# The stick-breaking key sums as two one-pass triangles, the new x turned by transposes, and a shorter Newton step

## What is computed

```python
# branch A, stick-breaking attention, 6 heads of 64, z = q.k * scale (query x key)
log_beta = log_sigmoid(z)
log_one_minus = where(past, log_sigmoid(-z), 0.0)
between = cumsum(log_one_minus, axis=keys, reverse=True) - log_one_minus
a = where(past, exp(log_beta + between), 0.0)
...
x = x + g1 * rms_norm(y, g_post_mix)
h = rms_norm(x, g_pre_ffn) * (1.0 + sc2) + sh2      # the "new x", normed
y = swiglu(h, w_up, w_down)
x = x + g2 * rms_norm(y, g_post_ffn)
```

## Time and profile before

| | |
|---|---|
| median of 3 runs | 461.66 us (461.51 to 461.84) |
| profiled execution, its own time | 461.65 us |
| its span | 459.9 us |
| granted TensorE clock, mean | 0.997 of full |
| TensorE busy | 444.4 us, 97% |
| VectorE busy | 328.5 us, 71% |
| ScalarE busy | 239.2 us, 52% |
| POOL busy | 34.9 us, 8% |
| the six triangles on `tri` (line 1708), with the six on `neg1` (line 1709) | 12 and 12 records, 126.7 to 167.1 us |
| the turns of x (line 1647) | 32 records, 258.6 to 272.1 us |

### The profile page before, as it was taken

One profiled execution on the slowest core, in us unless ns is written; L12 is line 12 of the kernel. 1 busy time (PEld: TensorE's weight loads), 2 busy tenths in 40 slices (PEclk: granted clock), 3 DMA queues, 4 the chain that ended last, 5 costly groups with the idle time before them and its releaser, 6 DMA issues.

```text
span 459.9 us, 7891 instructions
## 1 busy us (share of the span) xinstructions
PE 444.4 (97%) x2982; PEld 390.7 (85%) x2982; DVE 328.5 (71%) x587; ACT 239.2 (52%) x417; POOL 34.9 (8%) x77
## 2 busy tenths in 40 slices
PE   4899999999999999999999999999999999999994
PEld 3678988999999889989997899888888888888883
DVE  4724668786987868856995685796596587678645
ACT  4513884656756655596563576433534525425331
POOL 2000102000322231000000001000000000000000
PEclk9999999999999999999999999999999999999998
DMA  8999466886787657746669425988648557530002
GB/s 289 383 376 331 150 230 224 278 286 238 254 289 275 218 152 273 239 144 201 192 204 370 162 78 166 378 300 276 223 162 288 188 195 261 182 137 0 0 0 91
DMA packets 61634, 99.86 MB, mean 217 GB/s; under 512 B 3892, under 2 KB 44452, under 8 KB 61604
## 3 DMA queue, kind: packets, MB, share of 16 engines
q1 hardware_dynamic: 56480, 81.57, 52.5%
q0 software_dynamic: 4960, 17.84, 11.2%
q10 hardware_dynamic: 164, 0.05, 0.0%
HBM read 98.40 MB, written 1.05 MB: 216 GB/s over the span
## 4 chain that ended last, share of the span: by engine, by line
PE 91%; DVE 4%; issue 2%; ACT 2%; DMA 1%; SPq 0%; DVEq 0%; ACTq 0%
PE psum L1552 17%; PE psum L1951 16%; PE psum L1553 16%; PE psum L1554 16%; PE psum L1952 8%; PE psum L1614 3%; PE psum L1898 3%; PE psum L1568 2%; PE psum L1737 1%; DVE wlo L1094 1%; DMA xt<-in_x_dram 1%; PE psum L1676 1%; PE psum L1674 1%; PE psum L1708 1%; PE psum L1647 1%
## 5 line engine op out<-in xcount | busy, mean ns | idle before, releaser
L1951 PE MATMUL psum<-hcut,whi 128*128 128x512 f32 x320 | 113.6, 399 | 0.0
L1952 PE MATMUL psum<-hcut,wlo 128*128 128x256 f32 x320 | 89.9, 281 | 0.0
L1552 PE MATMUL psum<-hcut,whi 128*128 128x256 f32 x280 | 82.3, 294 | 0.3 <-DVE wlo L1094 0.3
L1553 PE MATMUL psum<-hcut,whi 128*128 128x256 f32 x280 | 79.1, 283 | 0.0
L1554 PE MATMUL psum<-hcut,wlo 128*128 128x256 f32 x280 | 79.1, 282 | 0.0
L1094 DVE TENSOR_TENSOR wlo<-raw,whi 128x768 fp32r<-128x768 f32 (+3 forms) x68 | 64.3, 972 | 19.1 <-ACT whi L743 18.8
L1951 PEld LDWEIGHTS psum<-hcut,whi 128*128 128x128 f32 x320 | 60.1, 188 | 14.9
L1952 PEld LDWEIGHTS psum<-hcut,wlo 128*128 128x128 f32 x320 | 60.5, 189 | 0.4
L743 ACT ACTIVATE whi<-raw 128x768 fp32r<-128x768 f32 (+3 forms) x68 | 55.6, 850 | 6.6 <-PE psum L1862 3.2
L1552 PEld LDWEIGHTS psum<-hcut,whi 128*128 128x128 f32 x280 | 53.4, 191 | 5.5 <-ACT qk L822 2.0
L1553 PEld LDWEIGHTS psum<-hcut,whi 128*128 128x128 f32 x280 | 53.5, 191 | 0.0
(11 more groups left out here) (245 smaller groups left out, 823.9 us busy)
## 6 DMA issues: line engine op xcount, KB each, us to landing
raw<-in_w_up_dram SPq DMA_DIRECT2D x22, 1024.0 KB, 7.6
xn<-in_w_ada_dram POOLq DMA_DIRECT2D x32, 512.0 KB, 5.2
raw<-in_w_in_dram SPq DMA_DIRECT2D x6, 2048.0 KB, 9.1
draw<-in_w_down_dram SPq DMA_DIRECT2D x11, 1024.0 KB, 5.0
ada<-in_w_ada_dram SPq DMA_DIRECT2D x16, 384.0 KB, 9.3
raw<-in_w_in_dram SPq DMA_DIRECT2D x3, 1536.0 KB, 8.8
raw<-in_w_o_dram SPq DMA_DIRECT2D x8, 512.0 KB, 5.2
raw<-in_w_in_dram SPq DMA_DIRECT2D x3, 1280.0 KB, 6.7
```

Source lines behind the costliest of these rows:

```text
L1552: pe.matmul(dst, a[0], b[0], start=first, stop=False)
L1553: pe.matmul(dst, a[0], b[1], start=False, stop=False)
L1951: pe.matmul(dst[:, :], wh, hcut[:, k, :, :].rearrange("p a s -> p (a s)"), start=k == 0, stop=False)
L1952: mm = pe.matmul(dst[:, S:2 * S], wl, hhi[:, k, :], start=False, stop=k == KC - 1)
```

## The change

Three parts. **Sums:** `tri` becomes float32r, a float32r copy `neg_all` of `neg1` is made by ScalarE at the start, and the masked softplus is cut into high part (ScalarE, into the place of `bufa[n % 2]`) and rest (VectorE, in the place of `bufp[n % 2]`). The two float32 matmuls become four float32r ones: each of the two parts by `tri` and by `neg_all`. -1 and 0 have no rest, so nothing is lost on their side. `second` waits for `sp_lo` in place of `sp_masked`. As `bufa` is now in use until the sums are made, two waits on `sums` are added. **New x:** `scale_new_x` replaces `spread_root`. VectorE scales the first 512 columns of the new x and ScalarE the last 512, into `xn`, and `turn_x` transposes the eight chunks of `xn`. **Newton:** ScalarE makes -var/2 by one more single-column Copy after its root, and VectorE's three instructions become two.

```diff
--- before.py
+++ after.py
@@ -292,7 +292,6 @@
         xn = sb("xn", [P, TT, D])
         hx = xn[:, :, :].rearrange("p t (k n) -> p t k n", n=P)
         ada_part = [xn[:, t, :] for t in range(TT)]
-        diag = [xn[:, t, D - P:D] for t in range(TT)]
         gpart, gsum = [xn[:, t, :] for t in range(TT)]
         h32 = xn[:, :, :].rearrange("p t (k n) -> p (t k) n", n=S)
         ident = sb("ident", [P, P])
@@ -306,7 +305,7 @@
         ssq = sb("ssq", [P, 8, 2])
-        var, root_, rinv = (sb(name, [P, 8]) for name in ("var", "root", "rinv"))
+        var, minus_half, root_, rinv = (sb(name, [P, 8]) for name in ("var", "minus_half", "root", "rinv"))
         warm = sb("warm", [P, 1])
         grow = [None, sb("grow1", [KC, P])]
         ones = sb("ones", [P, P], F32R)
@@ -324,7 +323,8 @@
         mrow = sb("mrow", [P, BANK], scope=mix)
         dist = sb("dist", [P, CAUSAL], scope=mix)
         dsel = sb("dsel", [P, CAUSAL], scope=mix)
-        tri = sb("tri", [P, P], scope=mix)
+        tri = sb("tri", [P, P], F32R, scope=mix)
+        neg_all = sb("neg_all", [P, P], F32R, scope=mix)
         neg1 = sb("neg1", [P, P], scope=mix)
         vec_rows = sb("vec_rows", [VEC_END, P], scope=mix)
         score = sb("score", [P, CAUSAL], scope=mix)
@@ -351,10 +351,17 @@
+
+
+        cut_part = ExitStack()
+        sb("cut_pad", [P, TT * D + (3 * KC + N_OCH + FULL_OCH) * S + 2 * D + BANK + 4 * CAUSAL + 4 * P + 2 * TT * 8 + VEC_END],
+           scope=cut_part)
+        sp_cut = [[sb(f"sp_{name}{i}", [P, CAUSAL], F32R, scope=cut_part) for i in range(2)] for name in ("hi", "lo")]
+        cut_part.close()
         start = ExitStack()
         ada = sb("ada", [P, KC, 2, ADA_COLS], scope=start)
...
@@ -641,15 +648,14 @@
             pool.wait_ge(consts, 1)
             pool.affine_select(out=ident[:, :], in_=ident[:, :], compare_op=ALU.not_equal, fill=1.0,
                                base=0, pattern=[[-1, P]], channel_multiplier=1).then_inc(ident_ready, 1)
-            pool.memset(tri[:, :], -1.0).then_inc(consts, 1)
             pool.memset(neg1[:, :], -1.0).then_inc(consts, 1)
             pool.iota(bufa[0][:, 0:P].bitcast(mybir.dt.int32), pattern=[[1, P]], base=0, channel_multiplier=-1).then_inc(consts, 1)
             pool.iota(bufa[0][:, P:CAUSAL].bitcast(mybir.dt.int32), pattern=[[1, 2 * P]], base=-P, channel_multiplier=-1).then_inc(consts, 1)
-            pool.wait_ge(consts, 5)
-            pool.affine_select(out=tri[:, :], in_=tri[:, :], compare_op=ALU.is_ge, fill=0.0,
+            pool.wait_ge(consts, 4)
+            pool.affine_select(out=tri[:, :], in_=neg1[:, :], compare_op=ALU.is_ge, fill=0.0,
                                base=0, pattern=[[-1, P]], channel_multiplier=1).then_inc(consts, 1)
             pool.tensor_copy(dist[:, :], bufa[0][:, :].bitcast(mybir.dt.int32)).then_inc(consts, 1)
-            pool.wait_ge(consts, 7)
+            pool.wait_ge(consts, 6)
             for c0 in (0, 2 * P):
                 pool.affine_select(out=dist[:, c0:c0 + P], in_=dist[:, c0:c0 + P], compare_op=ALU.is_ge, fill=MASKED,
                                    base=0, pattern=[[-1, P]], channel_multiplier=1).then_inc(consts, 1)
@@ -764,6 +770,7 @@
                 act.wait_ge(var_ready, j + 1)
                 act.activation(root_[:, j:j + 1], var[:, j:j + 1], ACT.Sqrt).then_inc(sqrt_ready, 1)
+                act.activation(minus_half[:, j:j + 1], var[:, j:j + 1], ACT.Copy, scale=-0.5).then_inc(half_ready, 1)
             def load_roots():
@@ -879,8 +886,9 @@
                     act.activation(chunk_view(whi, end_hi, k), chunk_view(raw, None, k), ACT.Copy).then_inc(w_hi, 2)
                     chunk_h_hi(k)
                 if k == 2:
-                    act.wait_ge(consts, 3)
+                    act.wait_ge(consts, 2)
                     act.activation(ones[:, :], neg1[:, :], ACT.Copy, scale=-1.0).then_inc(ones_set, 1)
+                    act.activation(neg_all[:, :], neg1[:, :], ACT.Copy).then_inc(ones_set, 1)
                 if k == KC - 1:
                     act.preload_act_table_set("natural_log_exp_and_others")
             for q in range(4):
@@ -902,11 +910,15 @@
                     z = bank[z_place(n)][:, 0:CAUSAL]
                     e = bufa[n % 2][:, :]
                     if n >= 2:
-                        act.wait_ge(sp_ready if n - 2 in SB_NO else p_ready, (SB_NO[n - 2] + 1) if n - 2 in SB_NO else SOFT_NO[n - 2] + 1)
+                        act.wait_ge(sums if n - 2 in SB_NO else p_ready, (SB_NO[n - 2] + 1) if n - 2 in SB_NO else SOFT_NO[n - 2] + 1)
                     then(act.activation(e, z, ACT.Abs))
                     then(act.activation(e, e, ACT.Exp, scale=-1.0))
                     act.activation(e, e, ACT.Ln, bias=1.0).then_inc(ln_ready, 1)
                 take_unit(u)
+                if u in NORM_AT and NORM_AT[u] in SB_NO:
+                    n = NORM_AT[u]
+                    act.wait_ge(sp_masked, 2 * (SB_NO[n] + 1))
+                    act.activation(sp_cut[0][n % 2][:, :], bufp[n % 2][:, :], ACT.Copy).then_inc(sp_hi, 1)
                 if u in LOGIT_PAIR_AT:
                     for h in (2 * LOGIT_PAIR_AT[u], 2 * LOGIT_PAIR_AT[u] + 1):
@@ -1015,13 +1027,20 @@
                     square_sum(3 + 2 * t, n, xt[:, t, BANK * n:BANK * (n + 1)], squares[n])
                 root(3 + 2 * t)
+            def scale_new_x(t):
+                j = 3 + 2 * t
+                act.wait_ge(rinv_ready, t + 1)
+                act.activation(xn[:, t, BANK:D], xt[:, t, BANK:D], ACT.Copy, scale=rinv[:, j:j + 1]).then_inc(xn_other, 1)
+
             squares = [f[:, :, :].rearrange("p j n -> p (j n)") for f in flo]
             norm_y(0, 0)
             norm_new_x(0)
+            scale_new_x(0)
             second_up_hi(0)
             norm_y(0, 1)
             norm_new_x(1)
             second_up_hi(2)
+            scale_new_x(1)
             second_up_hi(3)
             modulate(1)
             for t in range(TT):
@@ -1101,7 +1120,7 @@
             def inverse_root(j, meanwhile=lambda: None):
-                v, r, t = var[:, j:j + 1], rinv[:, j:j + 1], root_[:, j:j + 1]
+                v, half, r, t = [a[:, j:j + 1] for a in (var, minus_half, rinv, root_)]
                 dve.wait_ge(ss_ready, 2 * j + 1)
                 then(dve.tensor_scalar(v, ssq[:, j, 0:1], 1.0 / D, EPS, ALU.mult, ALU.add))
                 dve.wait_ge(ss_ready, 2 * j + 2)
@@ -1109,13 +1128,14 @@
                 meanwhile()
                 dve.wait_ge(sqrt_ready, j + 1)
                 then(dve.reciprocal(r, t))
-                then(dve.tensor_scalar(t, v, r, r, ALU.mult, ALU.mult))
-                then(dve.tensor_scalar(t, t, -0.5, 1.5, ALU.mult, ALU.add))
-                then(dve.tensor_scalar(r, r, t, None, ALU.mult))
-
-            def spread_root(j, t):
-
-                dve.tensor_scalar(diag[t], ident[:, :], rinv[:, j:j + 1], None, ALU.mult).then_inc(xn_ready, 1)
+                dve.wait_ge(half_ready, j - 1)
+                then(dve.tensor_scalar(t, half, r, r, ALU.mult, ALU.mult))
+                then(dve.tensor_scalar(r, t, 1.5, r, ALU.add, ALU.mult))
+
+            def scale_new_x(j, t):
+
+                dve.sem_inc(rinv_ready, 1)
+                dve.tensor_scalar(xn[:, t, 0:BANK], xt[:, t, 0:BANK], rinv[:, j:j + 1], None, ALU.mult).then_inc(xn_ready, 1)
             def modulate(t):
@@ -1318,6 +1338,11 @@
                     for t, (c0, c1) in enumerate(((0, P), (P, CAUSAL))):
                         ins = dve.tensor_scalar(bufp[n % 2][:, c0:c1], bufp[n % 2][:, c0:c1], ssum[:, n % 2, t:t + 1], None, ALU.mult)
                     ins.then_inc(p_ready, 1)
+                if u in NORM_AT and NORM_AT[u] in SB_NO:
+                    n = NORM_AT[u]
+                    dve.wait_ge(sp_hi, SB_NO[n] + 1)
+                    dve.tensor_tensor(sp_cut[1][n % 2][:, :], bufp[n % 2][:, :], sp_cut[0][n % 2][:, :].bitcast(F32),
+                                      ALU.subtract).then_inc(sp_lo, 1)
                 if u in EXP_AT and EXP_AT[u] in SB_NO:
                     n = EXP_AT[u]
                     z = bank[z_place(n)][:, 0:CAUSAL]
@@ -1337,8 +1362,10 @@
                     i = SOFT_NO[n]
                     slope = SLOPES[2 * h + (branch == "ds")]
                     dve.wait_ge(z_ready, n + 1)
+                    if n - 2 in SB_NO:
+                        dve.wait_ge(sums, SB_NO[n - 2] + 1)
                     if n == 0:
-                        dve.wait_ge(consts, 9)
+                        dve.wait_ge(consts, 8)
                     for t, (c0, c1) in enumerate(((0, P), (P, CAUSAL))):
                         ins = dve.tensor_tensor_reduce(bufa[n % 2][:, c0:c1], z[:, c0:c1], reach(n)[:, c0:c1], 1.0, LOWEST,
...
@@ -1465,7 +1492,7 @@
             for t in range(TT):
                 add_residual(0, t)
                 inverse_root(3 + 2 * t)
-                spread_root(3 + 2 * t, t)
+                scale_new_x(3 + 2 * t, t)
                 for q in ((0,), (2, 3))[t]:
```

(24 more changed lines are left out.)

## The result

Before: 461.75 us (461.51 to 462.00, 4 runs). After: **456.89 us** (456.20 to 457.79, 4 runs). The ratio is 0.9896, with a 95% interval of 0.9878 to 0.9914. That is faster. The profiled execution after took 456.9 us with a span of 455.2, where the one before had 461.65 and 459.9.

A forecast was written before the change was run, and what follows sets the result against it. TensorE, busy 97% of the span, was taken to bound the kernel. Gains of 1.75 (sums), 0.90 (first turn), 0.45 (second turn) and 0.19 (end) made 3.29: 461.65 - 3.29 = 458.36, forecast 458.4 us, range 457.5 to 459.9.

The forecast's parts named there:

- What bounds the kernel: Whole kernel: TensorE bounds it, busy 97% of the span; what leaves its stream comes off the time.
- The sums: Each head's tri and neg1 matmuls: 0.87 us becomes 0.58, so six heads gain 1.75 us.
- the straight line of 0.07: Float32r matmul of 128 columns in the sums: 0.07 us as lower estimate, from 256 and 384 columns; 0.115 was taken.
- the triangle waits for nothing: Copy and subtraction before each head's triangle end in time, 0.6 us spare at the last head; wait costed at nothing.
- slow narrow matmuls: Rival, in the sums: a 128-column float32r matmul takes 0.22 us like float32, giving 459.6; chance 0.15.
- a waiting triangle: Rival, in the heads: TensorE waits for the triangle's operand; mild 460.2, chance 0.07; heavy 464.4, chance 0.04.
- The first turn: First turn of x: eight transposes take 0.88 us for sixteen records' 1.78, with no wait; gain 0.90.
- turns that give nothing or more: Two rivals, both turns: transposes at 0.22 us each, 459.7, chance 0.04; or at 0.056 each, 457.5, chance 0.02.
- The second turn: Second turn of x: 0.90 us less, 0.45 given back waiting for ScalarE (0.25) and VectorE (0.2); gain 0.45.
- The tail: Behind TensorE's last product: the last tile's Newton step loses one instruction, 0.19 us, without waiting for the halved variance.
- The sum: Whole kernel: gains total 3.29 us, giving 458.4 us; forecast's chance 0.68.
- a sign that it would be wrong: Any stage without edits: a change of its length by over 0.3 us would show the prediction wrong.

The follow-up runs named there:

- turn: The scaling of the new x and the transposes alone, on the kernel before: 461.26 us, ratio 0.9985.
- after_noshift: The kernel after, with the halved variance kept in spare columns of the existing tile crep so that no tile moves: 458.3 us, ratio 0.9909.
- newton_noshift: The Newton part alone on the kernel before, with the halved variance in the existing tile crep so that no tile moves: 461.66 us, ratio 0.9982.

## Why the prediction was right in its parts and wrong in its sum

**What bounds the kernel:** held. TensorE's stream got shorter and the end followed, with 97% and 91% on it as before.

**The sums:** held. 0.58 a head was forecast and 0.57 measured; the product behind the sixth head starts 1.38 ahead of before, and it had started 0.41 behind: 1.79, where 1.75 was forecast. That is luck in part, as the split was wrong and cancelled: the 128-column matmul takes 0.05 (134.71 to 134.76), less than the straight line of 0.07, and the 384-column one that follows it 0.23 in place of 0.17. Together they are 0.28, against 0.285 in the sum. That the triangle waits for nothing held too: 0.68 of cover was measured at the last head, 0.6 forecast. The rivals of slow narrow matmuls and of a waiting triangle fall.

**The first turn:** held, 0.89 against 0.90. The eight records took 0.88 and were followed at once by the next product. VectorE's half took 0.49 (0.45 forecast). ScalarE's took 0.71, above the 0.63 that I gave as its most, and nobody waited for it there. The factor of four that the Trainium skill gives (TensorE: Matmul & The Clock Gate, Terms) isn't what this chip shows: 16 records in 1.78 became 8 in 0.88, a factor of two, as the three lone transposes had said. The rivals of turns that give nothing or more fall: eight transposes in a row ran at 0.11 each, and the granted clock was 1.00 in the stretches of both turns (257.3 to 258.3 and 268.1 to 269.1), so the 2.4 GHz level. What the Trainium skill says of transposes and the clock gate (TensorE: Matmul & The Clock Gate, Part 4) cost nothing here. All transposes of these runs stand amid products, so the rule itself isn't tested.

**The second turn:** held in mechanism, 0.38 against 0.45. The wait for ScalarE's chunk 0 was 0.27 (0.25 forecast), and what follows lost 0.25 (0.2). `turn` shows how thin it is: with the longer Newton step 0.08 is left of it.

**The tail:** held, 0.19 against 0.19. The halved variance was ready before the reciprocal began and was never waited for.

**The sum is where it failed.** These terms measured 1.79 + 0.89 + 0.38 + 0.19 = 3.25, and the forecast was 3.29. But the Newton part was costed by its instructions alone. Its new tile of 32 bytes, which I costed at nothing by not naming it, moved all that was allocated behind it. The up-products of the FFN became faster by 2.0 us, in a stage without edits; the prediction named that as a sign that it would be wrong. 1.8 of it, the nine later steps, is shown to be the tile's; the 0.2 of the first step is open. Start-up gave 0.4 back, within what executions differ by. 461.65 - 3.25 - 1.99 + 0.41, plus 0.1 lost between the sixth head and the first turn, is the 456.9 of the profiled execution. The range had no room for it, since it was made only of the bounds of the named costs. `after_noshift` is the change as I had costed it, and its profile has no gain in the loop. That its 458.3 us fall on the forecast to 0.1 is luck in part, since the kernel before was slower in that set of runs (462.23) than the 461.65 of the forecast.

Two things don't quite close. Measured by ratios, `after_noshift` gained 4.2 us (3.4 to 4.9), more than the 3.29 forecast, and its profile shows 2.95 from the first triangle to the last product and some 0.2 in the tail. `newton_noshift` gained 0.8 where its profile shows 0.2. So some 1.0 us of the one and 0.6 of the other isn't attributed. It may belong to the Newton part, which both have, or to the scatter between programs.

## What to carry to other kernels

An added or removed tile is part of a change, however small: it moves every tile allocated behind it, and here 32 bytes were worth 1.8 us of 460, as much as the largest of the edits. Before an edit is credited or blamed, look at the stages that it doesn't touch, and compare with a version whose tiles stay in place; a spare tile at two or three offsets costs nothing to try. Where TensorE is the bound, terms taken as distances between starts in the nearest rows came out within 0.1 us each, one of them with an error that cancelled.

## What the runs showed of the hardware

- The pace of float32r products depends on where tiles lie that they don't use. From the second step on, a pair of 512 and 256 columns took 0.353 us with `flo` in its old place and 0.347 with it 32 bytes further. The slower pace is a rhythm in which every third pair takes 0.361. The down part between two steps took 5.83, and 5.95 where `flo`, or `fhi` and `flo`, moved and `dhi` and `dlo` did not. No wait shows in either.
- A float32r matmul of 128 columns between two of 384 starts the next one after 0.05 us, less than half of the 0.12 of 256 columns, and the next takes 0.23 in place of 0.17: the pair counts, 0.28.
- A float32 transpose of 128x128 took 0.11 in a row of eight as in a row of three, half of a float32 matmul of that shape.
